# The states of four mLSTM heads: one product turned with the normaliser as a 129th column, one store for all

## The reference, cut to what matters

```python
w_state = jnp.exp(b[..., -1:] - b + ig - m_new[..., None])
decay = jnp.exp(b[..., -1] + m - m_new)
C_new = decay[..., None, None] * C + jnp.einsum('bhs,bhsv,bhsd->bhvd', w_state, v, k)
n_new = decay[..., None] * n + jnp.einsum('bhs,bhsd->bhd', w_state, k)
```

## Time and profile before

| | |
|---|---|
| median of 3 runs | 664.78 us (664.69 to 665.74) |
| the profiled execution | 665.21 us, span 663.5 us |
| mean granted TensorE clock | 0.995 |
| PE busy | 635.4 us (96%) |
| DVE busy | 350.5 us (53%) |
| ACT busy | 151.8 us (23%) |
| POOL busy | 207.0 us (31%) |

### The profile page before, as it was taken

How to read it: one execution, slowest core, us unless ns; L and a number is a source line. 1 busy time by engine, 2 the same in 40 slices (tenths; PEclk the granted TensorE clock), 3 DMA queues, 4 the chain that set the end, 5 groups by cost and what they waited for, 6 DMA issues and landing times.

```text
span 663.5 us, 8673 instructions
## 1 busy us (share of the span) xinstructions
PE 635.4 (96%) x3244; PEld 389.2 (59%) x3244; DVE 350.5 (53%) x801; ACT 151.8 (23%) x333; POOL 207.0 (31%) x243
## 2 busy tenths in 40 slices
PE   6999999999999999999999999999999999999993
PEld 3445588887787774446888774444574444333331
DVE  0283356327457792657653865355873324244365
ACT  1113311002524230002001740221324111121144
POOL 4141010100476566411100986002243432111221
PEclk9999999999999999999999999999999999999997
DMA  8994478613344345002904987555448999999797
GB/s 300 392 329 167 143 172 225 235 42 127 100 134 157 103 161 192 17 0 81 364 0 137 337 300 275 208 206 191 175 161 346 413 408 416 389 363 413 275 198 156
DMA packets 45811, 146.14 MB, mean 220 GB/s; under 512 B 5738, under 2 KB 6058, under 8 KB 41663
## 3 DMA queue, kind: packets, MB, share of 16 engines
q1 hardware_dynamic: 31847, 108.55, 43.6%
q0 software_dynamic: 11744, 32.24, 17.2%
q10 hardware_dynamic: 2176, 4.76, 1.9%
HBM read 130.34 MB, written 20.33 MB: 227 GB/s over the span
## 4 chain that ended last, share of the span: by engine, by line
PE 81%; DMA 9%; DVE 4%; issue 2%; ACT 1%; POOL 1%; ACTq 0%; DVEq 0%; POOLq 0%
PE ps L606 15%; PE ps L753 14%; PE ps L515 9%; PE ps L481 8%; PE ps L1093 7%; PE ps L1113 4%; PE ps L604 4%; DMA P<-x_d,smp 3%; DMA xn<-y_d 2%; PE ps L854 2%; PE ps L778 2%; PE ps L662 2%; PE ps L838 1%; PE ps L677 1%; PE ps L543 1%
## 5 line engine op out<-in xcount | busy, mean ns | idle before, releaser
L753 PE MATMUL ps<-wring,P 128*128 128x512 f32 x224 | 99.2, 596 | 0.0
L753 PEld LDWEIGHTS ps<-wring,P 128*128 128x128 f32 x224 | 41.6, 190 | 49.1 <-issue 49.0
L1093 PE MATMUL ps<-wring,P 128*32 128x512 f32 (+1 forms) x288 | 63.6, 593 | 0.9 <-DVE P L2355 0.9
L1779 DVE SCALAR_TENSOR_TENSOR P<-ps,P 128x264 f32<-128x264 f32 (+1 forms) x70 | 28.8, 427 | 60.9 <-PE ps L606 44.2
L515 PE MATMUL ps<-wring,P 128*128 128x512 f32 x128 | 57.9, 610 | 1.0 <-DVE P L1734 0.8
L481 PE MATMUL ps<-xT,wring 128*128 128x312 f32 (+1 forms) x256 | 56.8, 383 | 0.0
L2522 POOL TENSOR_SCALAR rstd<-agg 128x1 f32<-128x1 f32 (+1 forms) x15 | 16.8, 1120 | 114.7 <-DVE agg L1719 114.6
L481 PEld LDWEIGHTS ps<-xT,wring 128*128 128x128 f32 x256 | 46.6, 190 | 9.3
L2355 DVE COPY P<-ps 128x512 f32<-128x512 f32 x11 | 7.6, 692 | 74.5 <-PE ps L1074 74.5
L515 PEld LDWEIGHTS ps<-wring,P 128*128 128x128 f32 x128 | 24.6, 196 | 31.0 <-issue 30.8
L1093 PEld LDWEIGHTS ps<-wring,P 128*32 128x32 f32 (+1 forms) x288 | 21.6, 128 | 35.0 <-issue 34.9
(11 more groups left out here) (445 smaller groups left out, 1104.0 us busy)
## 6 DMA issues: line engine op xcount, KB each, us to landing
wring<-in_w_in SPq DMA_DIRECT2D x5, 2048.0 KB, 9.8
wring<-in_w_gate SPq DMA_DIRECT2D x10, 1024.0 KB
wring<-in_w_up SPq DMA_DIRECT2D x10, 1024.0 KB
P<-in_w_down SPq DMA_DIRECT2D x10, 1024.0 KB, 12.1
P<-in_cache_mem_k SPq DMA_DIRECT2D x8, 1024.0 KB, 6.3
P<-in_cache_mem_v SPq DMA_DIRECT2D x8, 1024.0 KB, 5.5
y_d<-P POOLq DMA_DIRECT2D x1, 4160.0 KB, 31.7
wring<-in_ca_wv SPq DMA_DIRECT2D x2, 2048.0 KB, 20.8
```

Source lines behind the costliest of these rows:

```text
L753: last = mm(bk[:, :], src[:, k, START[t]:START[t] + TR], w[:, k, :], start=(k == 0), stop=(k == KC - 1))
L1093: last = mm(GU[p % 2][lo:lo + m, :].rearrange("p (g f) -> p g f", g=2), xgT[:, p % 3, k, lo:lo + m], gu[s][:, :, k, :], start=(k == 0), st ...
L1779: V.scalar_tensor_tensor(dst, src, scale, part, ALU.mult, ALU.add).then_inc(part_added, 1)
```

## The change

The operands of the state product change places: `kw` is the weight, and `vn` with its ones column moves, 129 columns, so that one group of four products gives k by v with the normaliser as the 129th column. VectorE copies the 128x128 part to `stateT[:, h]` (four slots in `gb[:, 1, 0:512]`) and the column to `state_n[:, h]`. Nothing is stored until all heads are done. Then, between wo0 and wo1, TensorE turns the four parts back into one bank of RING_A, ACT copies them to `stateC`, and GpSimd stores `state_n` (128 partitions of 4 values, k by h in SBUF, h by k in DRAM) and `stateC`. The ln1 vectors are loaded ahead of these stores, after a wait for the turn. ACT waits for both stores before `copy_first("wq0")`, whose results overwrite the place.

```diff
-        Cout = gb[:, 1, 0:512].rearrange("p (b k) -> p b k", b=2)
+        stateT = gb[:, 1, 0:512].rearrange("p (h v) -> p h v", h=H)
+        stateC = view(13012, 512, "p (h k) -> p h k", h=H)
+        state_n = view(12244, H)
...
                 for i in range(NQT):
-                    mm(bk[:, 0:HD], vn[:, i, h, 0:HD], kw[:, i, :], start=(i == 0), stop=(i == NQT - 1))
-                for i in range(NQT):
-                    last = mm(bk[0:1, HD:2 * HD], vn[:, i, h, HD:HD + 1], kw[:, i, :], start=(i == 0), stop=(i == NQT - 1))
+                    last = mm(bk[:, 0:HD + 1], kw[:, i, :], vn[:, i, h, :], start=(i == 0), stop=(i == NQT - 1))
...
+            def turn_states():
+                pe.wait_ge(dve_free, at["state", 3])
+                bk = bank_a()
+                for h in range(H):
+                    last = nc.tensor.transpose(bk[:, h * HD:h * HD + HD], stateT[:, h, :], ident)
+                last.then_inc(act_full, 1)
+                at["states"] = na[0]
...
                     if k == 2:
-                        pe.wait_ge(act_free, na[0])
+                        pe.wait_ge(act_free, at["pool"])
...
                 if name == "wo0":
                     transpose_heads(3, head_bank)
+                    turn_states()
...
-            for i in range(2):
-                sp.wait_ge(c_out[i], 64)
+            sp.wait_ge(c_out, 32)
...
+            def take_states():
+                bk = full()
+                A(stateC, bk[:, :].rearrange("p (h k) -> p h k", h=H), ACT.Copy).then_inc(act_free, 1)
...
+            take_states()
             for t in range(3):
                 take_x(t)
             take_sample_rows(mixed_rows)
             at["mixed rows"] = nf[0]
 
+            act.wait_ge(c_out, 32)
             copy_first("wq0", CE ** -0.5)
...
                 bk = full()
-                if h >= 2:
-                    dve.wait_ge(c_out[h % 2], 32)
-                V.tensor_copy(Cout[:, h % 2, 0:HD], bk[:, 0:HD])
-                V.tensor_copy(Cout[0:1, h % 2, HD:2 * HD], bk[0:1, HD:2 * HD]).then_inc(dve_free, 1)
+                V.tensor_copy(stateT[:, h, :], bk[:, 0:HD])
+                V.tensor_copy(state_n[:, h:h + 1], bk[:, HD:HD + 1]).then_inc(dve_free, 1)
...
-            def state_out(h):
-                pool.wait_ge(dve_free, at["state", h])
-                pool.dma_start(o_pC[0, 0, h], Cout[:, h % 2, 0:HD]).then_inc(c_out[h % 2], 16)
-                pool.dma_start(o_pn[0, 0, h:h + 1], Cout[0:1, h % 2, HD:2 * HD]).then_inc(c_out[h % 2], 16)
+            def states_out():
+                pool.wait_ge(dve_free, at["state", 3])
+                pool.dma_start(o_pn[0, 0].rearrange("h k -> k h"), state_n, allow_slow_non_contiguous=True).then_inc(c_out, 16)
+                pool.wait_ge(act_free, at["states"])
+                pool.dma_start(o_pC[0, 0].rearrange("h v k -> v h k"), stateC).then_inc(c_out, 16)
...
                 load_state(2 * h + 3)
-                state_out(h)
                 head_rstd(h + 1, TR, NQT)
                 masks(h + 2)
-            state_out(2)
...
             head_rstd(3, TR, NQT)
-            state_out(3)
             update_state(6)
...
-            for i in range(2):
-                pool.wait_ge(c_out[i], 64)
+            pool.wait_ge(act_full, at["states"])
             norm_vectors("ln1_g", "ln1_b")
+            states_out()
             load_state(7)
```

More of the change, by code:

```diff
@@ L325, in layer_kernel @@
         mb_full, wexp_done, sel_done = sem("mb_full"), sem("wexp_done"), sem("sel_done")
-        c_out, un_out, sn_out = [sem(f"c_out{i}") for i in range(2)], sem("un_out"), sem("sn_out")
+        c_out, un_out, sn_out = sem("c_out"), sem("un_out"), sem("sn_out")
         sig_done = sem("sig_done")
```

## The result

The changed kernel took 672.92 us (median of 6 executions, 669.03 to 674.02), the kernel before beside it 665.54: a ratio of 1.0083, 95% interval 1.0055 to 1.0112. Executions more than 1.5% above the fastest of the same kernel count neither in a ratio nor in a mean: one each of e5 (676.05 us), e6 (1352.81) and e7 (677.67). The prediction, 664.9 with a range to 666.5 and 0.12 for slower, was wrong. The profiled execution took 671.20 us with a span of 669.5, against 665.21 and 663.5.

The account below looks back on a forecast made before the run. TensorE holds 81% of the chain, but VectorE was taken to limit each head's stage. Copies -0.33 and turn +0.44 sum to +0.11 us: 665.3 from the profiled 665.21, 664.9 by the median; range 663.0 to 666.5.

Parts of the forecast that it names:

- The sum of the head stage: mLSTM heads through the turn: VectorE's copies -0.33 us, turn +0.44, together +0.11 us; the removed row's time becomes waits.
- the column copy: VectorE's 128x1 copy replacing the 269 ns row copy: taken as 0.15 us, giving -0.33 us over heads 0 to 2.
- the turn: Four transposes added on TensorE between wo0 and wo1: +0.44 us on the path, bounds 0.42 and 0.60.
- Rival 1: Behind the states TensorE, not VectorE, sets the pace, so the whole row's saving comes through: -3.40 us, 661.4; chance 0.08.
- rival 2: Only head 3's row saving comes through, the pooling products not being held by pool_diff(0): -0.85 us, 663.9; chance 0.05.
- What covers this: Step after the heads: load_state(7) 0.1 to 0.2 us later; residual rows 0 covered by 5.3 us, their bank by 4.2.
- rival 3: The normalisers' 4-byte store blocks GpSimd's queue ahead of load_state(7): if 10.5 us, excess 3.7 us, 668.6; chance 0.08.
- threshold of 6.8 us: Time the normalisers' store must exceed before delaying load_state(7) shows at all, that load having until 275.3 us to land.
- what this is worth: Step on the state products: the removed row's 0.96 us a head, read from where TensorE next waits; itself gains nothing.
- So the saved 0.96 turns into a wait of about 0.9: Heads 0 to 2: TensorE reaches score 2 about 0.96 us sooner, then waits about 0.9 us for VectorE.

Follow-up runs that it names:

- e5: The changed kernel with the normalisers turned and stored as rows (as in e4), both stores moved behind update_state(7): ratio 1.0026, +2.4 us.
- e6: The kernel before with one 256 KB store of 512-byte rows to a spare tensor added in front of load_state(7): ratio 0.9995, -0.4 us.
- e7: The changed kernel with update_state(6) moved behind the ln1 vector loads, so these go out earlier, the states' stores following behind it: ratio 1.0044, +2.8 us.
- e3: The kernel before with one store of 512 separate floats to a spare tensor added between the ln1 vectors and load_state(7): ratio 1.0064, +4.3 us.
- e4: The changed kernel with the normalisers turned on TensorE too and stored as 4 rows of 512 bytes, same place in the queue: ratio 1.002, +1.9 us.
- e2: The changed kernel with the 256 KB state store moved behind update_state(7), the normalisers' store left in place: ratio 1.0038, +2.2 us.
- e11: The changed kernel run once more, unedited, against the kernel before: ratio 1.0089, +5.5 us.
- e1: The changed kernel with the normalisers' store moved behind update_state(7): ratio 1.0027, +2.6 us.
- e18: The kernel before without the normaliser row product, a second run of the same kernel as e13: ratio 1.0056, +3.7 us.
- e13: The kernel before without the normaliser row product, no other edit: ratio 1.0038, +2.3 us.
- e14: The kernel before with the merged product, and the row product again behind it into an unread part of the bank: ratio 0.9999, +0.3 us.
- e16: The kernel before with VectorE's state copy and next masking products put ahead of head_norm1 for heads 0 and 1: ratio 0.9988, +0.1 us.

## Why the prediction was wrong

**The sum of the head stage was right.** The row product's time turned into waits for VectorE of the size forecast, the column copy took 148 ns for 150, the turn 0.43 to 0.44 us, and the projection began 0.28 us later, 0.06 counted from head 0, for the 0.11 summed. For the column copy the Trainium skill (VectorE: DVE Perf Modes, the section on the TRN2 errata) gives an estimate of 126 ns; the trace has 22 more. Rival 1 (the whole row comes through) and rival 2 are out: the pooling products waited 1.0 us for L1995.

**The step that failed first** is "What covers this", with rival 3 beside it. I let the normalisers' store delay only what is issued behind it, load_state(7), and gave that 10 us of cover; rival 3's price and its threshold of 6.8 us were made on that load too. I kept the ln1 vectors out, since they are issued ahead. In three profiles of four the second of them landed 10.8 to 12.2 us after issue instead of 5.5 to 6.5, within 1.7 us of the store behind it, and its own cover was 4.2 us, counted with an issue at 258.00 that in this profile came at 259.32. Rival 3's 10.5 us for the store was close to what was measured, 10.9 to 12.1. What it had at 0.08 was the likely course: the row of 32-byte pieces was the wrong measure for 4-byte ones. The rule of the Trainium skill (DMA: Bandwidth & Descriptors, Rules for kernel authors) that a non-contiguous last dimension becomes one descriptor for each element spoke against the store. That such a store is slow is what e3 and e4 bear out (12.1 us against 5.9 for the same bytes in rows); how many descriptors it became is in no trace. The profile of e3 has 45843 packets for the 45811 of the kernel before, 32 more, and not the 512 that rival 3 counted.

**The second thing left out** is what a late landing does behind itself: behind the wait of some 2.2 us TensorE lost 1.9 us more to the clock. A wait was priced at its length alone.

**The step "what this is worth" of the state products** failed in its sign. "So the saved 0.96 turns into a wait of about 0.9" is what the trace shows, and I took it to be free. Taking the product away and doing nothing else makes the kernel slower by 0.38% and 0.56% on two chips, and 19 of 24 executions have the lower granted clock. Shown is that the removal does it, and that with work or instructions put back no loss is left that these runs can see; so the operands aren't needed for it, nor is the turn, which alone cost 0.8 us (0.9993 to 1.0031). Not shown is whether it is TensorE's idle behind each state or the smaller number of instructions, nor by which way it reaches stages 200 us later. The idle doesn't do it on the spot: the granted clock in the heads is 1.00.

**The terms together**: store about +3 (e3 alone 4.3, e2 nothing), removal +2 to 2.5 by what is left without the store and 2.3 to 3.7 by itself, turn +0.43, copy -0.33 to -0.38 by the length of the stage, against +5.5 measured. The first two are known to about 1.5 us each, so that they add up is no proof of them.

## What to carry to other kernels

Keep a store of single floats away from loads on which TensorE waits, in the same queue; ask not only what is issued behind it but what is still in flight ahead of it, or turn the data first so that it goes out in rows. Before work is taken off TensorE, look at what it waits for next: if another engine sets the pace there, nothing is gained, and here something was lost. A cover of 4 us in one profile is not a margin when the same load is issued up to 3 us later in other executions and lands 5 us later beside a store of floats, and a difference of 0.3% needs the distribution of executions, for which a profile is no substitute.

## What the runs showed of the hardware

A store of 512 separate floats, 2 KB, took 10.9 to 12.1 us to land where the change put it (after, e2, e3, e11), 8.0 us in e7 and 8.5 us in e1; the same data in 4 rows of 512 bytes took 5.9 us (e4), and a 256 KB store in rows of 512 bytes at this place 6.2 us (e6). A load of 512 KB issued 0.5 us ahead of it in the same queue landed after 10.8 to 12.2 us in three profiles of four; the one issued 1.1 us ahead landed after 5.0 to 5.6 us in all. While it ran, the DMA engines were busy for 0.69 of a window at 41 GB/s (after, 266 to 268 us), with other transfers in flight.

Behind waits of 2.2 to 2.4 us (the idle of TensorE in after and in e3) and of 1.7 us (e18) TensorE ran for some 3.4 us at or near half clock; behind idles of 0.6 to 1.1 us (the heads in after and e13, the last cached V in before) the granted clock stayed at 1.00. It fell too, from 496 us in after and e18 and from 492 in e14 and e16, with TensorE busy throughout. The executions of the kernel before spread over 664.5 to 670.6 us.
